# The second norm of a decoder layer: x transposed by quarters inside the output projection, the reciprocal root multiplied in as a row, the first two up units interleaved

## The reference

```
sh1, sc1, g1, sh2, sc2, g2 = split(silu(c) @ w_mod + b_mod)    # six vectors of 2048
hm = rms_norm(x) * (1 + sc1) + sh1
x  = x + g1 * mlstm_mixer(hm)         # w_in, 8 heads, w_out (2048 x 2048)
hf = rms_norm(x) * (1 + sc2) + sh2    # rms_norm(x) = x * rsqrt(mean(x*x) + 1e-6), per token
x  = x + g2 * conv_ffn(hf)            # w_up (2048 x 11264), conv over 3 tokens, silu(gate)*val, w_down
```

## Time and profile before

| | us |
|---|---|
| median of 3 runs (1255.99 to 1257.72) | 1257.47 |
| the profiled execution | 1256.31 |
| its span, first to last instruction | 1254.4 |
| PE busy in the span | 1183.7 |
| DVE busy | 943.8 |
| ACT busy | 577.1 |
| POOL busy | 193.7 |

### The profile page before, as it was taken

The page is one execution under the profiler, slowest core; times in us unless marked ns, Lnnn a source line. Parts: engine busy times, 40 slices in busy tenths (PEclk is TensorE's granted clock), DMA queues, the critical chain, the costliest instruction groups (busy, mean ns, idle before and its releaser), DMA issues.

```text
span 1254.4 us, 20909 instructions
## 1 busy us (share of the span) xinstructions
PE 1183.7 (94%) x7646; PEld 1082.0 (86%) x7646; DVE 943.8 (75%) x952; ACT 577.1 (46%) x756; POOL 193.7 (15%) x184
## 2 busy tenths in 40 slices
PE   2299999999999994999999999999999999999998
PEld 2288999877878874999999888999999889999986
DVE  6898978798888896798888556666776556666763
ACT  3245465555554444444444443444444344444432
POOL 0000020001121212121122112211221111211221
PEclk9599999999999896999999999999999999999999
DMA  9889999898889993689996566666665666666552
GB/s 364 325 313 401 400 315 379 308 373 305 319 331 349 363 304 94 187 265 284 276 263 234 199 193 178 181 186 187 181 170 199 201 192 177 175 194 182 186 196 73
DMA packets 260024, 313.50 MB, mean 250 GB/s; under 512 B 6056, under 2 KB 186728, under 8 KB 251272
## 3 DMA queue, kind: packets, MB, share of 16 engines
q1 hardware_dynamic: 259360, 312.51, 74.7%
q10 hardware_dynamic: 442, 0.21, 0.1%
q0 software_dynamic: 176, 0.16, 0.1%
HBM read 310.76 MB, written 2.10 MB: 249 GB/s over the span
## 4 chain that ended last, share of the span: by engine, by line
PE 83%; DVE 7%; DMA 6%; ACT 1%; issue 1%; POOL 0%; POOLq 0%; SPq 0%; DVEq 0%; ACTq 0%
PE ps L1110 13%; PE ps L1111 13%; PE ps L1112 13%; PE ps L1128 9%; PE ps L1130 9%; PE ps L1129 9%; DMA m<-in_l_w_mod_dram 5%; PE ps L1162 2%; PE ps L1163 2%; PE ps L1164 2%; DVE acc L870 2%; PE ps L1172 2%; PE ps L1174 2%; PE ps L1175 2%; DVE acc L852 1%
## 5 line engine op out<-in xcount | busy, mean ns | idle before, releaser
L839 DVE TENSOR_TENSOR w_lo<-raw,w_hi 128x1024 fp32r<-128x1024 f32 x392 | 516.9, 1330 | 164.4 <-ACT w_hi L553 164.0
L553 ACT ACTIVATE w_hi<-raw 128x1024 fp32r<-128x1024 f32 x392 | 414.1, 1057 | 403.3 <-PE ps L1130 182.6
L1110 PE MATMUL ps<-hm_hi,w_hi 128*128 128x256 f32 x1408 | 399.6, 284 | 8.7 <-DVE hm_lo L890 8.7
L1111 PE MATMUL ps<-hm_lo,w_hi 128*128 128x256 f32 x1408 | 399.4, 284 | 0.0
L1112 PE MATMUL ps<-hm_hi,w_lo 128*128 128x256 f32 x1408 | 399.3, 284 | 0.0
L1110 PEld LDWEIGHTS ps<-hm_hi,w_hi 128*128 128x128 f32 x1408 | 271.2, 193 | 9.0 <-issue 8.9
L1111 PEld LDWEIGHTS ps<-hm_lo,w_hi 128*128 128x128 f32 x1408 | 271.3, 193 | 0.1
L1112 PEld LDWEIGHTS ps<-hm_hi,w_lo 128*128 128x128 f32 x1408 | 271.3, 193 | 0.0
L1128 PE MATMUL ps<-w_hi,act_hi 128*128 128x512 f32 x352 | 137.4, 390 | 0.0
L1129 PE MATMUL ps<-w_lo,act_hi 128*128 128x512 f32 x352 | 137.0, 389 | 0.0
L1130 PE MATMUL ps<-w_hi,act_lo 128*128 128x512 f32 x352 | 136.9, 389 | 0.0
(11 more groups left out here) (152 smaller groups left out, 1375.0 us busy)
## 6 DMA issues: line engine op xcount, KB each, us to landing
raw<-in_l_w_up_dram SPq DMA_DIRECT2D x88, 1024.0 KB, 5.8
mod_raw<-in_l_w_mod_dram SPq DMA_DIRECT2D x56, 1024.0 KB, 6.7
raw<-in_l_w_in_dram SPq DMA_DIRECT2D x96, 512.0 KB, 8.0
raw<-in_l_w_down_dram SPq DMA_DIRECT2D x44, 1024.0 KB, 5.0
m<-in_l_w_mod_dram SPq DMA_DIRECT2D x32, 640.0 KB, 7.2
raw<-in_l_w_out_dram SPq DMA_DIRECT2D x16, 1024.0 KB, 7.8
m<-in_l_w_mod_dram SPq DMA_DIRECT2D x16, 768.0 KB, 12.9
mod_wide<-in_l_w_mod_dram SPq DMA_DIRECT2D x8, 1024.0 KB, 7.0
```

The costliest lines, as they stand in the source:

```text
L553: nc.scalar.activation(w_hi[:, v % 4, :], raw[:, v // 2 % 4, (v % 2) * HALF:(v % 2 + 1) * HALF], ACT.Copy).then_inc(w_hi_made, 1)
L839: nc.vector.tensor_tensor(w_lo[:, v % 4, :], raw[:, v // 2 % 4, (v % 2) * HALF:(v % 2 + 1) * HALF], w_hi[:, v % 4, :].bitcast(f32), ALU.su ...
L1110: mm(out, hi, hm_hi[:, k, :], start=(k == 0), stop=False)
L1111: mm(out, hi, hm_lo[:, k, :], start=False, stop=False)
```

## The change

The raw x is transposed, a quarter at a time: quarters 0, 1 and 2 behind halves 18, 21 and 27 of the output projection, quarter 3 behind its end (`transpose_quarter`, 16 tiles each, into banks 2 and 3). ACT copies each feature tile out with the factor 1 + sc2 (`take_z`). The reciprocal root isn't applied before the transpose any more: DVE multiplies `ident` by it (`rstd_diag`), PE multiplies `ones` by that into bank 0, and every partition then holds the root of every token as a row. DVE multiplies each tile by this row (`normalise`), ACT adds the shift into `hm_hi`, and DVE makes `hm_lo` in one instruction (`shift_lo`). The last output unit runs its token tile 0 whole, then tile 1. DVE itself adds quarter 3 to x. The mean and the epsilon go into the squares' scale and a fifth column, so that POOL has the power alone, and its `clear_acc(5)` comes before it. The column sums of the shift go ahead of the row. The first two up units run side by side, k by k. Not shown below: renamed waits, and `add_y` and the DVE and ACT loops cut to match.

```diff
...
-        xn = place("xn", [P, TB, D], 184 * KB)
         sq_junk = place("sq_junk", [P, TB * QUARTER], 184 * KB)
-        ss_quarter = place("ss_quarter", [P, TB, 4], 192 * KB)
+        ss_quarter = place("ss_quarter", [P, TB, 5], 192 * KB)
+        rstd_diag = place("rstd_diag", [P, TB, P], 193 * KB)
...
+            nc.gpsimd.memset(ss_quarter[:, :, 4], EPS).then_inc(eps_set, 1)
+            with pool.Fori(0, 3) as i:
                 add_y(Y_OUT, i)
-            rstd_of_x(1)
             pool.wait_ge(colsum_done, 5)
             clear_acc(5)
+            pool.wait_ge(ss_summed, 1)
+            nc.gpsimd.tensor_tensor(rstd, ms, minus_half, ALU.pow).then_inc(rstd_made, 1)
...
+            def squares(q, t):
+                act.wait_ge(x_added, 2 + 2 * q + t + 1)
                 if q:
-                    act.wait_ge(sq_made, TB + 2 * q)
-                for t in range(TB):
-                    nc.scalar.activation(sq_junk[:, t * QUARTER:(t + 1) * QUARTER],
-                                         x[:, t, q * QUARTER:(q + 1) * QUARTER],
-                                         ACT.Square, accum_out=ss_quarter[:, t, q:q + 1])\
-                             .then_inc(sq_made, 1)
+                    act.wait_ge(sq_made, TB + 2 * (q - 1) + t + 1)
+                nc.scalar.activation(sq_junk[:, t * QUARTER:(t + 1) * QUARTER],
+                                     x[:, t, q * QUARTER:(q + 1) * QUARTER], ACT.Square,
+                                     scale=float(D) ** -0.5, accum_out=ss_quarter[:, t, q:q + 1])\
+                         .then_inc(sq_made, 1)
...
+            def take_z(q):
+                act.wait_ge(xT_ready, KT // 2 + q + 1)
+                for j in range(4):
+                    k = 4 * q + j
+                    nc.scalar.activation(xnT[:, k, :],
+                                         ps[:, 2 + j // 2, (j % 2) * SEQ:(j % 2 + 1) * SEQ],
+                                         ACT.Copy, scale=scale_p[:, k:k + 1]).then_inc(z_made, 1)
...
             for f in range(33):
+                if f == 31:
+                    squares(3, 0)
+                if f == 32:
+                    squares(3, 1)
+                    scale_shift(4, 6, ps[:, 1, 0:KT], shift_p[:], False)
+                    act.wait_ge(sc_made, 6)
                 slot_hi(V_OUT + f)
...
+                if f in (20, 23, 29):
+                    take_z((20, 23, 29).index(f))
...
-            act.wait_ge(rstd_made, 2)
-            for q in range(4):
-                nc.scalar.activation(xn[:, 0, q * QUARTER:(q + 1) * QUARTER],
-                                     x[:, 0, q * QUARTER:(q + 1) * QUARTER], ACT.Copy,
-                                     scale=rstd[:, 0:1]).then_inc(xn_made, 1)
-            copy_xT(1)
-            scale_shift(4, 6, ps[:, 0, 0:KT], shift_p[:], False)
-            act.wait_ge(sc_made, 6)
-            for g in range(KT // 2):
-                if g % 2:
-                    act.wait_ge(xT_copied_v, KT // 4 + g // 2 + 1)
-                else:
-                    act.wait_ge(xT_copied, KT // 4 + g // 2 + 1)
-                modulate_hi(1, 2 * g, 2 * g + 2)
+            for k in range(KT):
+                if k == 3:
+                    take_z(3)
+                act.wait_ge(t_made, k + 1)
+                nc.scalar.activation(hm_hi[:, k, :], xnT[:, k, :], ACT.Identity,
+                                     bias=shift_p[:, k:k + 1]).then_inc(hm_hi_made, 1)
...
+            last = slice(3 * QUARTER, 4 * QUARTER)
+            for t in range(TB):
+                if t == 0:
+                    dve.wait_ge(y_last, 1)
+                else:
+                    dve.wait_ge(half_done, V_OUT + 32)
+                dve.wait_ge(x_added, 2 * (Y_OUT + 3) + t + 1)
+                nc.vector.tensor_tensor(y_tmp[:, t, :], ps[:, 6 + t, :], g_bc[:, last], ALU.mult)\
+                         .then_inc(y_scaled, 1)
+                dve.wait_ge(y_scaled, 4 + 2 * (Y_OUT + 3) + t + 1)
+                nc.vector.tensor_tensor(x[:, t, last], x[:, t, last], y_tmp[:, t, :], ALU.add)\
+                         .then_inc(x_added, 1)
+            split_lo(V_OUT + 34)
+            dve.wait_ge(eps_set, 1)
             dve.wait_ge(sq_made, TB + 4 * TB)
-            nc.vector.reduce_sum(ss, ss_quarter[:], mybir.AxisListType.X).then_inc(ss_summed, 1)
+            nc.vector.reduce_sum(ms, ss_quarter[:], mybir.AxisListType.X).then_inc(ss_summed, 1)
             dve.wait_ge(rstd_made, 2)
-            for q in range(4):
-                nc.vector.tensor_scalar(xn[:, 1, q * QUARTER:(q + 1) * QUARTER],
-                                        x[:, 1, q * QUARTER:(q + 1) * QUARTER], rstd[:, 1:2], None,
-                                        ALU.mult).then_inc(xn_made_v, 1)
-            copy_xT(1)
+            for t in range(TB):
+                nc.vector.tensor_scalar(rstd_diag[:, t, :], ident[:], rstd[:, t:t + 1], None, ALU.mult)\
+                         .then_inc(diag_made, 1)
+            def normalise(k):
+                dve.wait_ge(z_made, k + 1)
+                nc.vector.tensor_tensor(xnT[:, k, :], xnT[:, k, :], ps[:, 0, 0:SEQ], ALU.mult)\
+                         .then_inc(t_made, 1)
+            def shift_lo(k):
+                dve.wait_ge(hm_hi_made, KT + k + 1)
+                nc.vector.scalar_tensor_tensor(out=hm_lo[:, k, :], in0=xnT[:, k, :],
+                                               scalar=shift_p[:, k:k + 1], in1=hm_hi[:, k, :].bitcast(f32),
+                                               op0=ALU.add, op1=ALU.subtract).then_inc(hm_made, 1)
+            dve.wait_ge(rstd_row, 1)
             dve.wait_ge(sc_made, 6)
-            modulate_lo(1, 0, KT)
+            for k in range(KT + 2):
+                if k < KT:
+                    normalise(k)
+                if k >= 2:
+                    shift_lo(k - 2)
+                if k == 4:
+                    split_lo(V_OUT + 35)
...
+            def transpose_quarter(q):
+                pe.wait_ge(x_added, 2 + 2 * q + 2)
+                if q:
+                    pe.wait_ge(z_made, 4 * q)
+                else:
+                    pe.wait_ge(gated_made, 2 * H)
+                for j in range(4):
+                    k = 4 * q + j
+                    for t in range(TB):
+                        c0 = (j % 2) * SEQ + t * P
+                        last = nc.tensor.transpose(ps[:, 2 + j // 2, c0:c0 + P],
+                                                   x[:, t, k * P:(k + 1) * P], ident[:])
+                last.then_inc(xT_ready, 1)
+            def last_out_unit():
+                u, k0 = U_OUT + 15, 12
+                pe.wait_ge(raw_done, RAW0 + 2 * u + 2)
+                for t in range(TB):
+                    out = ps[:, 6 + t, :]
+                    for j in range(4):
+                        v, c0 = 2 * u + j // 2, (j % 2) * QUARTER
+                        hi, lo = w_hi[:, v % 4, c0:c0 + QUARTER], w_lo[:, v % 4, c0:c0 + QUARTER]
+                        s_hi = o_hi3[:, k0 + j, t * P:(t + 1) * P]
+                        s_lo = o_lo3[:, k0 + j, t * P:(t + 1) * P]
+                        mm(out, s_hi, hi, start=False, stop=False)
+                        mm(out, s_hi, lo, start=False, stop=False)
+                        last = mm(out, s_lo, hi, start=False, stop=(j == 3))
+                        if t and j % 2:
+                            last.then_inc(half_done, 1)
+                    if t == 0:
+                        last.then_inc(y_last, 1)
...
+                if r == 15:
+                    last_out_unit()
+                    continue
                 for half in range(2):
                     b_half(U_OUT + r, half, 4 + 2 * (q % 2), g, 4, o_hi3, o_lo3)
                     attend(V_OUT + 2 * r + half - V_VO)
+                    if 2 * r + half in (18, 21, 27):
+                        transpose_quarter((18, 21, 27).index(2 * r + half))
...
-            transpose_x(1)
+            pe.wait_ge(mod_done, 2 + 3 * KT)
+            pe.wait_ge(sc_made, 5)
+            column_sums(4, 1, 0, KT)
+            pe.wait_ge(diag_made, 2)
+            pe.wait_ge(o_made, 2 * H)
+            for t in range(TB):
+                last = mm(ps[:, 0, t * P:(t + 1) * P], ones[:], rstd_diag[:, t, :], start=True, stop=True)
+            last.then_inc(rstd_row, 1)
+            transpose_quarter(3)
             pe.wait_ge(y_scaled, 4 + 8)
-            pe.wait_ge(mod_done, 2 + 3 * KT)
-            pe.wait_ge(o_made, 2 * H)
-            column_sums(4, 0, 0, KT)
+            def first_up_units(u, a):
+                pe.wait_ge(a_free, a + 2)
+                pe.wait_ge(raw_done, RAW0 + 2 * u + 3)
+                for k in range(KT):
+                    pe.wait_ge(hm_made, KT + k + 1)
+                    if k == KT // 2:
+                        pe.wait_ge(raw_done, RAW0 + 2 * u + 4)
+                    for r in range(2):
+                        v, j = 2 * (u + r) + k // (KT // 2), k % (KT // 2)
+                        out = ps[:, 4 + (a + r) % 4, 0:SEQ]
```

(63 more changed lines are left out.)

21 lines of the change are left out of this document (7 added, 14 removed).

## The result

| | before | changed |
|---|---|---|
| median, us | 1257.6 (1255.99 to 1257.72, 4 runs) | 1239.59 (1238.51 to 1240.35, 4 runs) |
| profiled execution, us | 1256.31 | 1239.83 |
| its span, us | 1254.4 | 1237.9 |

The ratio is 0.9859 (95% interval 0.9842 to 0.9876): 18.0 us faster by the medians. The direction was right and the size was not. The forecast was 1244.6 with a range down to 1241, so the measured time lies outside it, with 12.9 us forecast.

The account below looks back on a forecast made before the run. PE bounds the kernel, busy 94%, so time can go only where it idles or is at low clock. Third up unit at 497.0 instead of 509.86: 12.9 us off 1256.31 gives 1243.4, plus 1.2 for the median 1244.6; range 1241 to 1252.

Parts of the forecast that it names:

- PE's idle stretch: Between the two projections, last output matmul to first up matmul, 25.7 us; with 3.5 us of low clock and waiting, 29.2 winnable.
- the mark: Start of the third up unit, behind which both kernels do the same; forecast at 497.0 instead of 509.86.
- Three groups of transposes inside the projection: Quarters 0 to 2 in the output projection: full cost 3 x 16 x 0.11 = 5.3 us, bounds 5.3 and 10.1.
- Quarter 3 is 16 transposes behind the row, 3.4 us: Last transposes, after the projection: 3.4 us at 0.21 each, 1.8 at 0.11; 3.4 taken.
- row begins: After the last output matmul: DVE can start on the row at 474.7 in trace time, bounds -1 and +2.5.
- DVE, a tile: DVE's 16 tiles behind the row: a multiply and a three-operand instruction, 0.80 us each, bounds 0.70 and 0.90.
- DVE's wait at tile 3: In DVE's tiles: `shift_lo(3)` waits for ACT, held by quarter 3's copies, a new wait of 1.2 us.
- A: Rival: the clock stays low through the first pair of up units, +6.9 us, 1251.5; chance 0.11.
- B: Rival: the clock falls behind each transposed group, 3 x 2.7 = 8.1 us, 1252.7; chance 0.06.
- C: Rival: low clock in the groups, behind them and in the pair, 19.8 us against 12.9 won, 1264.4; chance 0.04.
- D: Rival: longer chain of small hops, tiles at 0.90 and the row 2.5 late, +4.1 us, 1248.7; chance 0.13.
- E: Rival: the mark doesn't move, since transposes wait for x and PE loses inside what it wins behind; 1257; chance 0.03.

Follow-up runs that it names:

- e7: Changed kernel with only the last of the shift's 16 column sums made, the other 15 left out: 1238.98 us, ratio 0.9863.
- e5: Changed kernel with the last output unit in its old order, both token tiles ending together: 1241.33 us, ratio 0.9881.
- e8: Changed kernel with ACT splitting half 35 before it copies the shift, DVE making its low part while waiting for the row: 1238.99 us, ratio 0.9861.
- e10: As e8, with ACT's four copies of quarter 3 made one each ahead of tiles 3, 5, 7 and 9: 1238.72 us, ratio 0.9862.
- e4: Changed kernel with each group making its eight transposes twice, so 16: 1242.66 us, ratio 0.9888.
- e2: Changed kernel with the first up unit alone waiting tile by tile, the second following it as a whole: 1242.91 us, ratio 0.9888.
- e6: Changed kernel with POOL instead of DVE adding quarter 3 to x, as before the change: 1239.57 us, ratio 0.9864.
- e3: Changed kernel with all four groups of transposes behind the row, ACT's copies behind each: 1247.06 us, ratio 0.9926.
- e1: Changed kernel with the pair undone, the first two up units one after the other, each half waiting for eight tiles: 1246.01 us, ratio 0.9911.
- e9: Kernel before with the pair alone, its first two up units side by side, tile by tile: 1250.39 us, ratio 0.9951.
- e12: As e10, with the scale's column sums made four at a time behind halves 12 to 15 of the output projection: 1236.41 us, ratio 0.9843.
- e11: Changed kernel unaltered, measured again on the same chip as e9 to e12: 1239.78 us, ratio 0.9866.

## Why the prediction missed

**What held.** That PE's idle stretch is what shrinks, that its work stays the same, and the mark as the place to count to. That the groups inside the projection cost their full length and nothing waits for them (PE has no wait there, and the clock is 1.00). That tile 1's gate starts at the end of the last matmul (472.72, 0.03 behind it). That POOL's `clear_acc` ahead of its third wait is covered (it ends at 459.1, and DVE's sum, for which POOL waits next, starts at 475.19), and the column sums are too (e7). That DVE's tiles set the pair's end: the mark is 1.7 us behind DVE's last `hm_lo` in the changed kernel, e5, e8 and e10 alike.

**The step that failed: "Three groups of transposes inside the projection", 3 x 16 x 0.11 = 5.3 us, and "Quarter 3 is 16 transposes behind the row, 3.4 us".** A quarter is 4 feature tiles by 2 token tiles, that is 8 transposes; I counted 16, in the section on the change too, beside a diff whose loops make 4 x 2. The price of one, 0.10 to 0.11 us at the high clock and 0.21 at the low, was right. The measured terms are 2.7 and 1.9 us. The count could have been checked against a row: the old transposes of the whole x are 32 (`x32` in the earlier trace rows), so a quarter has 8. The two terms that enter the sum, 5.3 for the groups and 22.5 for the mark, were 5.2 us too long together (2.7 and 19.9 measured). e4, which makes 16, shows what of this is the miscount: its projection is 2.6 us longer (65.1 us from the scale's column sums on, 62.5 in e2, e5, e6, e7 and e10) and its mark 1.1 later, 3.7 us in its trace and 3.1 by the median. Between the profiled executions the forecast was off by only 3.6 us, 1243.4 against 1239.83: the 0.8 us ahead of the changed code and the 0.8 behind the mark, neither of them in the sum, went the other way. That these 1.6 us hide a third of the miss is luck.

**The rest are sizes.** By the terms of the sum, counted from the projection's end:

| term | forecast | measured |
|---|---|---|
| groups inside the projection | 5.3 | 2.7 |
| row begins | 4.4 | 4.0 |
| first up matmul | 8.9 | 6.9 |
| DVE, a tile | 0.80 | 0.73 |
| DVE's wait at tile 3 | 1.2 | 0 |
| last `hm_lo` ends | 20.7 | 18.2 |
| third up unit (mark) | 22.5 | 19.9 |

The tile was inside its bounds (0.70 to 0.90) and worth 1.1 us over 16 tiles. The column sums took 3.63 us at the high clock, where I had used the row that fell to the low one inside (4.33); so DVE's arm, not PE's, set the row. The wait at tile 3 didn't come, as quarter 3 was ready 1.5 us sooner (the miscount again: with 16 it is 1.01 us, e4) and ACT's copies take 0.39 us each (1.57 for four), not 0.565. With the right count it appears only once the split is out of the way (e8). The miscount and the tile's price added up in one direction, and the range's lower end, drawn from the tile and the row alone, left the count out.

**The rivals.** A (a low clock through the pair) was a real behaviour without a price. In the changed kernel the clock rises 0.3 us into the pair, in e7 2.7 us into it, and both marks are at 19.9. In e2 it stays low for nearly all of a unit. The Trainium skill, page "TensorE: Matmul & The Clock Gate", section "A second HAM failure mode: psum-queue depth-cycling", says that short idling of PE between groups makes the clock swing. The pair doesn't show it (1.00 in the whole window 480 to 490, with one wait of 0.70); e3, with waits of 1.75, stays at 0.50, but doesn't swing. B and C would need the clock to fall behind the groups; it didn't, not even at 16 (e4). D went the wrong way: the tile took 0.73 and not 0.90, and the row came early and not late. E needs transposes that wait for x; PE has no wait in the projection.

**What the parts are worth,** each undone alone: the groups' place 7.5 us (e3), the pair 6.4 (e1; 5.8 in the kernel before, e9), tile 0 first 1.7 (e5), DVE's add some 0.5 (e6). That is 16 of the 16 to 18 us, if they are taken as independent. The root as a row, which makes transposing the raw x possible, can't be undone alone without losing the groups' place, and was not tried; its own saving is part of the first figure.

## What to carry to other kernels

Move what doesn't depend on a late value ahead of that value: here the transposes cost 0.9 us a group in dense PE work and 3.7 in the chain. Where an engine makes tiles one by one, let PE work two units at once on each; it won some 6 us in both kernels. And count instructions against a row that has their number, before a price is put on them: the price was right to a hundredth, the count wrong by a factor of two.

## What the runs showed that I had not expected

A long row of narrow products brings the clock down, and in lots it doesn't. With the scale's 32 records in a row the granted clock falls to 0.50 within or behind them in every kernel but e12, where four lots of eight leave it at 1.00 and 2.3 us are won. How long it stays low differs between executions of like code. Where it falls well inside the records it is low for 6.8 us in all (the kernel before, the changed kernel, e1, e8, e11; the records then take 4.04 to 4.39 us). Where it falls at their end or behind it is low for 3.4 us (e2 to e7, e9, e10; 3.62 to 3.73 us). From the start of these sums to the end of the projection the changed kernel, e1, e8 and e11 take 64.1 us, where e2, e5, e6, e7 and e10, alike up to there, take 62.5; the kernel before takes 61.4, and e9, alike up to there, 59.8. So 1.6 us of one execution's time hang on where this fall comes. The two profiled executions compared above are both of the long kind.

A clock that is low where another engine is the bound costs nothing: e2 ran some 10 us of its first unit at 1.2 GHz, and its mark came where the sum at the high clock had put it, 4.5 us later for 4.7.
